# Differential attention as 32 written-out steps, values with tokens stationary, x's update and sums on VectorE

## The reference, cut to what matters

```
kv = rms_norm(x, kv_norm) @ w_kv                   # 1024 x 2048: k, then v
q  = rms_norm(x, b_norm_pre) @ w_q                 # 8 heads of two halves of 64
s  = q k^T per head and half, causal               # 512 x 512
a  = softmax(s_0) - lam * softmax(s_1)             # lam from b_lambda, one number
o  = rms_norm(a @ v per head (128 wide), subln) * (1 - lambda_init)
x  = x + rms_norm(o @ w_out, b_norm_post)
```

## Time and profile before

| | us |
|---|---|
| median of 3 runs | 3086.12 (3085.79 to 3087.54) |
| the profiled execution | 3084.02 |
| its span | 3082.2 |
| PE busy | 2847.0 (92%) |
| DVE busy | 1618.0 (52%) |
| ACT busy | 1248.2 (40%) |
| POOL busy | 224.2 (7%) |
| mean granted clock of TensorE | 0.963 of full |

### The profile page before, as it was taken

One profiled execution on the slowest core, in us unless ns is written; L12 is line 12 of the kernel. 1 busy time (PEld: TensorE's weight loads), 2 busy tenths in 40 slices (PEclk: granted clock), 3 DMA queues, 4 the chain that ended last, 5 costly groups with the idle time before them and its releaser, 6 DMA issues.

```text
span 3082.2 us, 35289 instructions
## 1 busy us (share of the span) xinstructions
PE 2847.0 (92%) x11944; PEld 2125.5 (69%) x11944; DVE 1618.0 (52%) x2215; ACT 1248.2 (40%) x1996; POOL 224.2 (7%) x197
## 2 busy tenths in 40 slices
PE   6999989999977888999997978999998899999999
PEld 4677766888854555688885646888876555678887
DVE  3323424777334544577623985555355576555532
ACT  3333333444324544444423654333234455533321
POOL 1000000000012000000002751000000121100000
PEclk9999999999988998999998989999999899999999
DMA  3222212333321111233331212333333100133332
GB/s 113 68 68 75 75 54 69 95 94 90 93 78 35 55 48 43 73 92 93 93 94 51 62 41 65 96 91 93 94 100 101 32 21 15 48 91 93 95 91 93
DMA packets 437485, 229.09 MB, mean 74 GB/s; under 512 B 7915, under 2 KB 436012, under 8 KB 437292
## 3 DMA queue, kind: packets, MB, share of 16 engines
q1 hardware_dynamic: 434992, 222.98, 25.0%
q10 hardware_dynamic: 2428, 5.28, 0.5%
HBM read 226.13 MB, written 2.10 MB: 74 GB/s over the span
## 4 chain that ended last, share of the span: by engine, by line
PE 80%; DVE 10%; ACT 5%; issue 2%; POOL 2%; ACTq 1%; DMA 0%; DVEq 0%; POOLq 0%; SPq 0%
PE lin L703 23%; PE lin L705 22%; PE lin L704 22%; PE stat L719 2%; DVE con_a L2122 2%; DVE w_lo L1720 1%; PE att L905 1%; PE lin L944 1%; PE att L777 1%; PE att L1090 1%; DVE y L1734 1%; PE lin L967 1%; ACT w_hi L1196 1%; DVE n_sm L2031 1%; PE att L769 1%
## 5 line engine op out<-in xcount | busy, mean ns | idle before, releaser
L1720 DVE TENSOR_TENSOR w_lo<-raw,w_hi 128x1024 fp32r<-128x1024 f32 x427 | 527.6, 1236 | 848.3 <-ACT w_hi L1196 836.6
L703 PE MATMUL lin<-xh,w_hi 128*128 128x512 f32 x2160 | 878.3, 407 | 26.6 <-POOL xl L634 23.5
L704 PE MATMUL lin<-xl,w_hi 128*128 128x512 f32 x2160 | 858.1, 397 | 0.0
L705 PE MATMUL lin<-xh,w_lo 128*128 128x512 f32 x2160 | 857.9, 397 | 0.0
L1196 ACT ACTIVATE w_hi<-raw 128x1024 fp32r<-128x1024 f32 x427 | 451.8, 1058 | 627.5 <-PE lin L705 615.0
L703 PEld LDWEIGHTS lin<-xh,w_hi 128*128 128x128 f32 x2160 | 407.9, 189 | 149.9 <-issue 27.8
L704 PEld LDWEIGHTS lin<-xl,w_hi 128*128 128x128 f32 x2160 | 408.6, 189 | 101.8 <-issue 7.3
L705 PEld LDWEIGHTS lin<-xh,w_lo 128*128 128x128 f32 x2160 | 408.0, 189 | 100.4
L703 PE MATMUL lin<-ffn_hi,w_hi 128*128 128x512 f32 x704 | 278.1, 395 | 0.0
L704 PE MATMUL lin<-ffn_lo,w_hi 128*128 128x512 f32 x704 | 278.1, 395 | 0.0
L705 PE MATMUL lin<-ffn_hi,w_lo 128*128 128x512 f32 x704 | 278.1, 395 | 0.0
(11 more groups left out here) (302 smaller groups left out, 3421.5 us busy)
## 6 DMA issues: line engine op xcount, KB each, us to landing
raw<-in_ffn_w_up SPq DMA_DIRECT2D x176, 512.0 KB, 3.8
raw<-in_ffn_w_down SPq DMA_DIRECT2D x64, 512.0 KB, 3.8
raw<-in_a_w_in SPq DMA_DIRECT2D x48, 512.0 KB, 3.9
raw<-in_ffn_w_down SPq DMA_DIRECT2D x32, 384.0 KB, 3.3
raw<-in_conv_w_pw SPq DMA_DIRECT2D x24, 512.0 KB, 3.9
raw<-in_nsa_w_in SPq DMA_DIRECT2D x21, 512.0 KB, 3.8
raw<-in_a_w_out SPq DMA_DIRECT2D x16, 512.0 KB, 3.9
raw<-in_w_kv SPq DMA_DIRECT2D x16, 512.0 KB, 3.9
```

The lines of the kernel that those rows point to most:

```text
L703: pe.matmul(bank, w_hi[s][:, k, :], h, start=start and k == 0, stop=False)
L704: pe.matmul(bank, w_hi[s][:, k, :], l, start=False, stop=False)
L705: done = pe.matmul(bank, w_lo[s][:, k, :], h, start=False, stop=stop and k == kc - 1)
L1720: dve.tensor_tensor(w_lo[s][:, :, :], raw[s][:, :, :], w_hi[s][:, :, :].bitcast(F32), ALU.subtract).then_inc(lo_done[s], 1)
```

## The change

- ffn0's close uses `then` with the keys' gain: VectorE adds x, makes `xl` and adds up the squares (`summed`); two weight splits come between its slices (`between`). TensorE starts on `xh`, `xl` unscaled; the rms `d_rs` is applied where the projections leave PSUM, and to v as a column `d_rc`, won by four transposes.
- ScalarE makes `xqh` from x, VectorE `xql`. GpSimd has no part in it.
- v is made first, for four heads at a time: a unit is now 256 rows by 512 columns; a 128-token block of xh is the stationary operand and 512 weight columns move; the four banks of `att` take the four token blocks. ScalarE copies them straight to `dif_v`. There is no `dif_vt` and no `turn_v`.
- The heads are 32 steps n (head n // 4, block n % 4), written out on each engine. Scores run two steps ahead. Units of q and k are cut in halves and put between the steps; the output projection's first two units in the last seven steps and behind them. A head's product with v goes to a `lin` bank, in the next head's first step; its rms, high and low part follow in steps 1 to 3.
- The difference folds lambda into one instruction. The function table is not loaded anew. b_lambda is loaded at the start, and lambda worked out in retention (in `acc`).

The diff at its core (queue loads; TensorE; ScalarE; VectorE's close; VectorE's steps):

```diff
+                def values(r):
+                    for u in range(4):
+                        s, t = units.take()
+                        sp.wait_ge(lo_done[s], t + 1)
+                        sp.sem_inc(slot_taken, 1)
+                        sp.dma_start(broad(raw[s]), a["w_kv"][u * 2 * P:(u + 1) * 2 * P, D + r * T:D + (r + 1) * T].rearrange(
+                            "(c p) n -> p c n", p=P)).then_inc(raw_full[s], 16)
+                def keys(h):
                     load(w_cols(a["w_kv"], 0, UC, h * P))
+                def queries(h):
                     load(w_cols(a["b_w_q"][0], 0, UC, h * P))
-                    load(w_cols(a["w_kv"], 0, UC, h * P + D))
-                head(0)
-                with rounds(sp, AH // 2 - 1, (units, 6)) as i:
-                    head(i * 2 + 1)
-                    head(i * 2 + 2)
-                head(AH - 1)
+                values(0)
+                keys(0)
+                keys(1)
+                values(1)
+                queries(0)
+                queries(1)
+                for h in range(2, AH):
+                    keys(h)
+                    queries(h)
...
+                def values(r):
+                    for u in range(4):
+                        s, t = units.take()
+                        pe.wait_ge(lo_done[s], t + 2)
+                        for c in range(2):
+                            k = 2 * u + c
+                            if r == 0:
+                                pe.wait_ge(xl_ready, first_ + k + 1)
+                            for b in range(TB):
+                                tok = slice(b * P, (b + 1) * P)
+                                if r and k == 0:
+                                    pe.wait_ge(d_v, b + 1)
+                                pe.matmul(att[:, b, :], xh[:, k, tok], broad(w_hi[s])[:, c, :], start=k == 0, stop=False)
+                                pe.matmul(att[:, b, :], xl[:, k, tok], broad(w_hi[s])[:, c, :], start=False, stop=False)
+                                done = pe.matmul(att[:, b, :], xh[:, k, tok], broad(w_lo[s])[:, c, :], start=False, stop=k == DC - 1)
+                        done.then_inc(unit_done[s], 1)
+                values(0)
+                sum_acc()
+                output(xh, xl, (UC,))
+                pe.wait_ge(d_rms, 1)
+                for b in range(TB):
+                    done = pe.transpose(trp[:, b, :], d_rs[:, b * P:(b + 1) * P], c_("ident"))
+                done.then_inc(d_rt, 1)
+                output(xh, xl, (UC,))
+                values(1)
+                output(xqh, xql, (UC,), lambda k: (xl_ready, first_ + DC + k + 1))
...
+                def scores(n):
+                    h, blk, sl = n // TB, n % TB, n % 2
+                    w = (blk + 1) * P
+                    if blk == 0:
+                        pe.wait_ge(d_k, h + 1)
+                        pe.wait_ge(d_q, h + 1)
+                    if n < 2:
+                        pe.wait_ge(d_v, TB + 2 * n + 2)
+                    else:
+                        pe.wait_ge(d_e, 2 * (n - 1))
                     for c in range(2):
-                        r = slice(c * 64, c * 64 + 64)
-                        done = pe.matmul(att[:, 2 * s + c, 0:w], dif_q[r, p, b * P:(b + 1) * P], dif_k[r, p, 0:w],
-                                         start=True, stop=True)
+                        r = slice(c * HD, (c + 1) * HD)
+                        done = pe.matmul(att[:, 2 * sl + c, 0:w], dif_q[r, h % 2, blk * P:w], dif_k[r, h % 2, 0:w], start=True, stop=True)
                     done.then_inc(d_s, 1)
...
+                dense("q1", 0, 4, xqh, xql)
+                scores(0)
+                scores(1)
+                last_n = AH * TB
+                for n in range(last_n):
+                    h, i = n // TB, n % TB
+                    if i == 0 and h + 1 < AH:
+                        dense(f"q{h + 1}", 4, 4, xqh, xql)
+                    if i in (1, 2) and h + 2 < AH:
+                        dense(f"k{h + 2}", 4 * (i - 1), 4, xh, xl)
+                    if i == 3 and h + 2 < AH:
+                        dense(f"q{h + 2}", 0, 4, xqh, xql)
+                    if n >= last_n - 7:
+                        k = n - (last_n - 7)
+                        if k < 6:
+                            dense("o0", k, 1, att_hi, att_lo)
+                    if n + 2 < last_n:
+                        scores(n + 2)
+                    if i == 0 and h:
+                        b, bt = banks.take()
+                        pe.wait_ge(bank_free[b], bt + 1)
+                        weigh(h - 1, lin[b])
+                    if i == 1 and h:
+                        sum_square(True, True)
+                    turn(n)
+                banks.take()
+                dense("o1", 0, 3, att_hi, att_lo)
+                pe.wait_ge(d_e, 2 * (last_n - 1))
+                weigh(AH - 1, att[:, 0, :])
+                dense("o1", 3, 2, att_hi, att_lo)
+                sum_square(True, True)
+                dense("o1", 5, 2, att_hi, att_lo)
+                dense("o0", 6, 1, att_hi, att_lo)
+                dense("o0", 7, 1, att_hi, att_lo)
+                dense("o1", 7, 1, att_hi, att_lo)
+                project(att_hi, att_lo, (8,), DC - 2)
...
+                for c in range(4):
+                    query_high(c)
+                split_next()
+                for c in range(4, DC):
+                    query_high(c)
+                act.wait_ge(sum_done, accs.next())
+                inverse_rms(D, dst=d_rs)
+                act.wait_ge(rs_ready, rss.last())
+                act.sem_inc(d_rms, 1)
+                split_next()
+                split_next()
+                act.wait_ge(d_rt, 1)
+                act.activation(d_rc[:, :], trp[:, :, 0], ACT.Copy).then_inc(d_col, 1)
+                act.wait_ge(d_col, 1)
+                place_values(0)
+                split_next()
+                for u in range(3):
+                    split_next()
+                s, t = multiplied()
+                place_values(1)
+                split(s, t)
+                split_next()
+                for _ in range(3):
+                    banks.take()
...
+                exps(0)
+                last_n = AH * TB
+                for n in range(last_n):
+                    h, i = n // TB, n % TB
+                    if n + 1 < last_n:
+                        exps(n + 1)
+                    if i == 0 and h + 1 < AH:
+                        split_next()
+                    if i == 0 and h:
+                        b, _t = banks.take()
+                        out_square(h - 1, lin[b][:, :])
+                    if i == 1 and h:
+                        out_rms()
+                    if i == 2 and h:
+                        out_high(h - 1)
+                    if i == 2 and h + 2 < AH:
+                        split_next()
+                    if i == 1 and h + 2 < AH:
+                        banks.take()
+                    if i == 3 and h + 2 < AH:
+                        banks.take()
+                    if n == last_n - 7:
+                        banks.take()
+                    place(n)
+                out_square(AH - 1, att[:, 0, :])
+                out_rms()
+                out_high(AH - 1)
+                project_out(dif_hT, 1, final, ("ffn_norm_pre", DC), 2)
...
-                        squares.next()
+                        if not summed:
+                            squares.next()
+                        elif c == 0:
+                            dve.memset(acc[:, :], 0.0).then_inc(acc_zero, 1)
+                            dve.wait_ge(acc_zero, zeros.next())
                         if c:
                             dve.wait_ge(x_ready, upd.n * DC + c)
                             lower_x(c - 1, *then)
+                            if summed:
+                                add_square()
+                        if c - 1 in between:
+                            split_next()
...
+                    dve.wait_ge(d_w, 2 * n + 1)
+                    if n >= 2:
+                        dve.wait_ge(d_tr, n - 1)
+                    dve.tensor_scalar(dif_a[:, s, 0:w], dif_e[:, s, 1, 0:w], inv_den[:, s, 1:2], neg_lam, ALU.mult, ALU.mult).then_inc(d_w, 1)
+                    dve.wait_ge(d_w, 2 * n + 2)
+                    dve.scalar_tensor_tensor(dif_a[:, s, 0:w], dif_e[:, s, 0, 0:w], inv_den[:, s, 0:1], dif_a[:, s, 0:w],
                                              ALU.mult, ALU.add).then_inc(d_a, 1)
...
+                top(0)
+                top(1)
+                last_n = AH * TB
+                for n in range(last_n):
+                    h, i = n // TB, n % TB
+                    difference(n)
+                    if n + 2 < last_n:
+                        top(n + 2)
+                    if i == 0 and h + 1 < AH:
+                        queries(h + 1)
+                    if i == 1 and h:
+                        b, _t = banks.take()
+                        out_normed(h - 1, lin[b][:, :])
```

(12 more changed lines are left out.)

318 lines of the change are left out of this document (137 added, 181 removed).

## The result

The kernel after takes 3006.34 us (median of four runs, 3003.97 to 3006.85) against 3086.51 (3085.79 to 3087.54): a ratio of 0.9738, 95% interval 0.9722 to 0.9755. The profiled execution takes 3006.15 us (span 3004.3) against 3084.02, so 77.9 us less. Predicted were 3005.6 us and 80.5 less.

A forecast was written before the change was run, and what follows sets the result against it. TensorE, 80% of the chain, bounds the kernel where it waits or is clocked low. Chain 87.5 us shorter, less 7 for the clock, gives 80.5 off 3084.0; with 2.1 for the median, 3005.6 us; range 2988 to 3034.

The forecast's parts named there:

- root to end of the first values: ffn0's close: first low part at 910.4, four value units 22.4 us, 1.8 for the low clock level, ending at 934.6.
- end: rest of head 7, output projection: Attention's end: 11.9 us after the last transposes, 1.7 waiting for a split, six units 33.6; together 47.2.
- The chain: ffn0's close to the last output unit: ends at 1168.9 against 1256.4, 87.5 us less at the full clock level.
- The clock term: New stretch: a mean granted clock of 0.97 over some 240 us of TensorE work costs 7 us more.
- the last output unit: Sign at the output projection's end: its last unit would come near 1169 to 1176.
- the scaled copies of v: Sign in the value units ahead of the heads: these copies would come near 943 and 972.
- A: Heads: TensorE waits in full for VectorE's evacuation and split before the difference, 28 us, giving 3034; chance 13%.
- B: New stretch: mean clock of 0.80, end at 1214, only 42 us less, giving 3044; chance 6%.
- D: New stretch: the clock stays low and the kernel is slower, 3114 at 0.65, 3226 at 0.5; chance 3%.
- C: Heads: written-out steps overlap no better than the old heads, only the front gains, 43 us, giving 3043; chance 5%.
- 2.8 and -0.2 us of slack: Steady head: transposes have 2.8 us of room after the query split; in the last step they wait 0.2 for the difference.
- the form of the values: Value units with xh as weights: same pitch as before, cost 0; upper bound 37 us at the low level's pitch.

The follow-up runs named there:

- e4: Kernel after with b_lambda's load and the lambda work put back in the attention, as in the kernel before: -0.10 us from the first y on, median 3003.66 us.
- e5: Kernel after with the low part of q's weights written twice in heads 1 to 6 (1.2 us more VectorE time each): 3.5 us slower.
- e6: Kernel after with the low part of k's weights written twice for heads 2 to 7 (1.2 us more VectorE time each): 10.2 us slower.
- e2: Kernel after with q and k projections as whole units behind steps 3 and 1, not halves: 30.6 us more to the attention's end, 27.3 to the kernel's end.
- e8: Kernel after with the second output unit's first three slices ahead of step 30's transposes, not behind them: 3.5 us less.
- e10: Kernel after with those three slices moved ahead of step 30's transposes and the phases' tiles 1 KB on: median 2997.26 us, 7.35 less from the first y on.

## Why the prediction was right

The time was right to 0.7 us. The gain forecast was 80.5 us; by the medians it is 80.2, by the profiled executions 77.9. Part of that closeness is chance: the profiled execution of the kernel before lies 2.5 us below its median, that of the kernel after 0.2. The mechanism was right: the gain comes from TensorE starting early in ffn0's close and from a filled pipeline in the heads. By the prediction's own steps, each measured from mark to mark (the first row is part of the second):

```
step                                    predicted   measured
root (first y) to first low part             4.0        4.3
root to end of the first values             28.2       29.3
from there to the first step                44.8       44.3
head 0                                      16.7       17.1
five heads                                  98.5       98.3
head 6                                      14.8       15.5
head 7                                      12.3       13.3
end: rest of head 7, output projection      47.2       49.0
in all                                     262.5      266.8
```

Where the 80.5 and the 77.9 part:

- **The chain.** It is 4.3 us longer than my sum had it, so 83.2 shorter than before and not 87.5. 1.1 is the first values: 0.3 up to the first low part, 0.6 because TensorE ran at a pitch of 0.43 for twelve matmuls (2.4 us more than at 0.233, where I had taken 1.8), 0.2 not followed further. 1.7 is heads 6 and 7, of which some 0.8 are the last seven transposes at the low level (0.90 and 1.09 long, where the same groups take 0.55 and 0.66 in a steady head) and the rest was followed too short. 1.8 is the end, and it is the clock: the nine matmuls between the last transposes and the last product take 3.9 us at the 0.43 pitch, where I had 2.1. The stretch between is 0.3 shorter.
- **The clock term** was the one that I placed wrongly. I took 7 us for a mean of 0.97 in the new stretch, beside the 1.8 for the first values. The mean was 0.96, but in the heads nothing was lost (1.00 from 935 to 1120): the losses stood at the two ends, 0.6 + 0.8 + 1.8 of the 4.3 above, and most of the 1.2 us between the last output unit and the next y, where the sum's matmul is at the low level (2.08 us at 1180.58). That is some 4.4 us, not 7. With the 1.1 us that the chain was short otherwise, the stretch gained 82.0 us, 1.5 more than the 80.5; the 4.0 us of the next point then made it 77.9. So the errors cancel in part, and the closeness of the total owes something to that.
- **The 4.0 us ahead of ffn0's first y**, which the prediction took to be unchanged, but for lambda's work. The first matmul of retention's output projection before, and the window of the clock behind it:

```profile
421.68 0.77 PE L703 MATMUL lin<-ret_hi,w_hi 128*128 128x512 f32 x1 [10.02 <-DVE ret_lo L1870]
```

```profile
425.00:435.00 10.00, 10.00 (x45) 8.03 (x44) 1.23 (x1) 1.62 (x2) 0.00 (x0) 1.00 0.18 54
```

The same two of the kernel after:

```profile
422.58 0.77 PE L720 MATMUL lin<-ret_hi,w_hi 128*128 128x512 f32 x1 [10.02 <-DVE ret_lo L1986]
```

```profile
425.00:435.00 10.00, 10.00 (x38) 7.92 (x37) 1.23 (x1) 1.06 (x1) 0.00 (x0) 0.82 0.01 3
```

This start is 421.4 to 426.3 among the nine kernels whose code is the same up to there, so 0.9 us is within chance. From it to the first addition to the sum are 15.0 us before and 16.3 to 16.5 in every kernel derived from the one after, e4 with lambda back included: after a wait of 10 us the clock rises later. Why always later, with one execution of before to compare, stays open. 0.3 and 0.4 are the tiles' place, 1.0 the last sum at the low level, where every kernel derived from the one after has it, too.

Of the signs that the prediction named, the last output unit came at 1177.3, just past its 1169 to 1176, by these 4.0 us; the scaled copies of v began at 947.5 and 974.8, not near 943 and 972.

The rivals. **A** (VectorE's extra work decides, 3034) did not happen, but e5 and e6 show how near it was: room for 1.2 us in one step, none in the other, where each further us of VectorE costs one in every head. The prediction's 2.8 and -0.2 us of slack stand: no wait in the first place, 0.24 us in the second. The other wait, 0.28 before the third step's transposes, it did not have. **B and D** (the clock) did not happen: 1.00 in the heads, 0.96 in the stretch. The Trainium skill, in "TensorE: Matmul & The Clock Gate", section "A second HAM failure mode: psum-queue depth-cycling", tells of a kernel that cycles through PSUM banks and whose clock swings, because of small idles between groups of matmuls. The trace does not show that for this kernel: eight banks in turn, waits of up to 0.5 us until head 6, and a granted clock of 1.00 from 935 to 1120 us. e2, with the same banks and a wait of 3.07 us in each head, shows 0.93; what differs between them is the waits, not the cycling. **C** (no better overlap) is refuted by 19.66 us a head against 30.7, and against the 25 that it named. The fair comparison is smaller, since v's unit (5.6 us a head) now stands ahead of the heads: 25.3 against 30.7. What carries the overlap is the order: with whole units a head takes 24.6 us, with the transposes ahead of scores, product and sum 22.0.

The edits that I costed at nothing were nothing: the form of the values (pitch 0.233 in both rows of units), the lambda work and the table loads (-0.1 and -0.07 us put back).

## What to carry to other kernels

Where a chain on other engines repeats beside one full engine, write the steps out and cut that engine's free work into pieces that stand exactly where the chain's waits are; here halves instead of whole units were worth 5 us in a head of 20, and transposes behind the scores, the product and the sum instead of ahead of them 2.3. Ask of each step, not of each loop, what room the second engine has: the same 1.2 us pass cost nothing in one step and its full length in another. Count the head and the tail of such a pipeline separately, since with less work to fill them their waits come back, and the lower clock level with them: here a wait of 2.9 us near the end was followed by matmuls at the 0.43 pitch, and moving three slices ahead of it (e8) removed both.

## What was unexpected in the hardware

Shifting the tiles that matmuls read by 128 bytes made those matmuls 0.4% slower (a round of 132 in 30.92 and not 30.80 us); a shift by 256 bytes or 1 KB did not. The matmuls of the same loops that read tiles that had not moved kept their pitch (a round of ffn0's first layer takes 11.20 us in both). Which operand or which rule of the address is behind it was not tried.

After the same 10 us wait, TensorE came back to its high level sooner or later (the granted clock of 425 to 435 us is 1.00 before and 0.82 after), and the sum's matmul behind a 3 us wait ran at either level (1.13 or 2.07 us at the same place of e8 and of e10). With this, one mark, the first addition to retention's sum, stood at 437.7 to 442.8 us in the nine kernels with the same code up to there, a scatter larger than several of the effects measured here.
